# A second block whose gates and branch projections are computed token-first with 512-wide weight rows

## What is computed

```python
def mixer_block(h, ...):                      # h: 256 x 1024
    zin = h @ w_in                            # ... the last 4096 columns are the gates
    ...
    branches = jnp.stack([o_a, o_b, o_c, o_d], axis=2)      # four of 256 x 256
    proj = jnp.einsum('bsnw,nwd->bsnd', branches, w_branch) # four of 256 x 1024
    gate = jax.nn.sigmoid(gates).reshape(b, s, N_BRANCH, D_MODEL)
    merged = jnp.sum(gate * proj, axis=2)                   # 256 x 1024
    return merged @ w_out
```

## Time and profile before

| | us |
|---|---|
| median of 3 runs (lowest, highest) | 2224.96 (2223.97, 2225.07) |
| profiled execution: span | 2222.8 |
| TensorE busy (share of the span) | 2189.5 (99%) |
| weight loads of TensorE (overlap its matmuls) | 2006.0 (90%) |
| VectorE busy | 1458.6 (66%) |
| ScalarE busy | 1114.8 (50%) |
| GpSimd busy | 52.3 (2%) |

### The profile page before, as it was taken

How to read it: one execution, slowest core, us unless ns; L and a number is a source line. 1 busy time by engine, 2 the same in 40 slices (tenths; PEclk the granted TensorE clock), 3 DMA queues, 4 the chain that set the end, 5 groups by cost and what they waited for, 6 DMA issues and landing times.

```text
span 2222.8 us, 36553 instructions
## 1 busy us (share of the span) xinstructions
PE 2189.5 (99%) x15888; PEld 2006.0 (90%) x15888; DVE 1458.6 (66%) x1616; ACT 1114.8 (50%) x1419; POOL 52.3 (2%) x46
## 2 busy tenths in 40 slices
PE   8999999999999999999999999999999999999998
PEld 7999998888899999788799999988889999998887
DVE  5778567555768757666677867456657786745664
ACT  5555645454564564544465445444445553544443
POOL 0000000000000000000000000000000000000000
PEclk9999999999999999999999999999999999999999
DMA  7645455565564555556545444456555544445553
GB/s 233 181 139 168 148 200 171 189 200 190 180 187 137 158 181 174 173 186 228 178 136 140 146 134 170 146 165 201 200 175 155 152 134 144 160 159 164 189 200 113
DMA packets 288614, 376.97 MB, mean 170 GB/s; under 512 B 22335, under 2 KB 240517, under 8 KB 288454
## 3 DMA queue, kind: packets, MB, share of 16 engines
q1 hardware_dynamic: 288454, 374.62, 53.2%
HBM read 368.10 MB, written 1.05 MB: 166 GB/s over the span
## 4 chain that ended last, share of the span: by engine, by line
PE 91%; DVE 6%; ACT 2%; issue 1%; DMA 1%; SPq 0%; POOL 0%; DVEq 0%; POOLq 0%; ACTq 0%
PE ps L611 17%; PE ps L2246 14%; PE ps L2817 7%; PE ps L621 5%; PE ps L2267 5%; PE ps L2257 4%; PE ps L1009 4%; PE ps L921 4%; PE ps L2325 4%; PE ps L623 3%; PE ps L2269 2%; PE ps L676 2%; PE ps L635 2%; PE ps L2314 2%; PE ps L961 1%; PE ps L937 1%
## 5 line engine op out<-in xcount | busy, mean ns | idle before, releaser
L1305 DVE TENSOR_TENSOR a_wlo<-a_ring,a_whi 128x2048 fp32r<-128x2048 f32 (+1 forms) x173 | 393.0, 2274 | 101.9 <-ACT a_whi L1035 101.4
L3152 DVE TENSOR_TENSOR b_wlo<-b_ring,b_whi 128x2048 fp32r<-128x2048 f32 (+1 forms) x168 | 379.6, 2262 | 109.6 <-ACT b_whi L2842 109.0
L1035 ACT CAST a_whi<-a_ring 128x2048 fp32r<-128x2048 f32 (+1 forms) x173 | 328.0, 1899 | 141.2 <-PE ps L921 48.7
L611 PE MATMUL ps<-a_nsp,a_whi 128*128 128x256 f32 x2144 | 387.3, 283 | 0.0
L2842 ACT CAST b_whi<-b_ring 128x2048 fp32r<-128x2048 f32 (+1 forms) x168 | 317.2, 1889 | 124.7 <-PE ps L2817 79.0
L611 PEld LDWEIGHTS ps<-a_nsp,a_whi 128*128 128x128 f32 x2144 | 334.1, 192 | 0.2
L611 PE MATMUL ps<-a_nsp,a_wlo 128*128 128x256 f32 x1072 | 306.3, 286 | 0.0
L2246 PE MATMUL ps<-b_nsp,b_whi 128*128 128x256 f32 x1568 | 284.7, 283 | 0.0
L2246 PEld LDWEIGHTS ps<-b_nsp,b_whi 128*128 128x128 f32 x1568 | 244.0, 191 | 0.1
L2246 PE MATMUL ps<-b_nsp,b_wlo 128*128 128x256 f32 x784 | 227.9, 291 | 0.9 <-DVE b_wlo L3152 0.9
L611 PEld LDWEIGHTS ps<-a_nsp,a_wlo 128*128 128x128 f32 x1072 | 205.5, 192 | 1.6 <-issue 1.0
(11 more groups left out here) (580 smaller groups left out, 4224.4 us busy)
## 6 DMA issues: line engine op xcount, KB each, us to landing
b_ring<-in_w_in SPq DMA_DIRECT2D x50, 1024.0 KB, 5.9
a_ring<-in_w_in SPq DMA_DIRECT2D x49, 1024.0 KB, 5.4
a_ring<-in_w_ffn_in SPq DMA_DIRECT2D x44, 1024.0 KB, 5.1
a_ring<-in_w_gate SPq DMA_DIRECT2D x32, 1024.0 KB, 5.5
b_ring<-in_w_up SPq DMA_DIRECT2D x32, 1024.0 KB, 5.4
b_ring<-in_w_down SPq DMA_DIRECT2D x32, 1024.0 KB, 5.0
a_ring<-in_w_ffn_out SPq DMA_DIRECT2D x22, 1024.0 KB, 4.9
a_ring<-in_w_branch SPq DMA_DIRECT2D x16, 1024.0 KB, 5.1
```

Of the source, the lines that this page charges most:

```text
L611: mm = T.matmul(out, w[:, k, c:c + P], x_[:, k, :], start=k == 0 and n == 0, stop=k == KD - 1 and n == 2)
L1035: nc.scalar.copy(part(whi, h), part(ring, h)).then_inc(hi_ok, 1)
L1305: nc.vector.tensor_tensor(part(wlo, h), part(ring, h), part(whi, h).bitcast(F32), ALU.subtract).then_inc(lo_ok, 1)
L3152: nc.vector.tensor_tensor(part(wlo, h), part(ring, h), part(whi, h).bitcast(F32), ALU.subtract).then_inc(lo_ok, 1)
```

## The change

The gates and the branch projections are computed token-first: the activations (128 tokens) are stationary and the weights move, 512 columns a matmul. `gates` and `merged` are now token-first, [128, 2 token tiles, 1024 features], in the same places. Two gate parts make a chunk of 512 gate columns: the first holds rows 0 to 511 of the weights, the second rows 512 to 1023, and both token tiles accumulate over the two parts in the two banks (`gate_rows`). ScalarE evicts both tiles behind the second. Of a branch, m now counts 512-column halves times token tiles. The sum is turned by TensorE (`merged_turn`, eight transposes for each half of the features), and its high and low pieces are read from PSUM. The memory's sixteen transposes move from behind part 30 into the output projection, in two groups of eight, behind its parts 1 and 2 (`memory_turn`).

```diff
-GATE_AT = {h: g for g, h in enumerate([*range(12, 20), *range(21, 25), *range(26, 30)])}
+GATE_AT = {h: (g // 2, g % 2) for g, h in enumerate([*range(12, 20), *range(21, 25), *range(26, 30)])}
...
-            parts += [(8, 256, lambda l, g=GATE_AT[h]: cols(a["w_in_2"], l, GATE2 + 256 * g, 256))]
+            parts += [(4, 512, lambda l, c=GATE2 + 512 * GATE_AT[h][0], r=GATE_AT[h][1]:
+                       rows(a["w_in_2"], l, 4 * P * r, 4)[:, :, c:c + 512])]
...
+        else:
+            c, r = GATE_AT[h]
+            used += [(full, filled["gate", c, 1]) if r else (half_used, c + 1)]
...
+        def gate_rows(h):
+
+            g, r = GATE_AT[h]
+            hi, lo = both(h)
+            pe.wait_ge(lo_ok, h + 1)
+            for t in range(NT):
+                if t:
+                    mid(h)
+                b = bank(("gate", g, t))
+                for kk in range(4):
+                    k = 4 * r + kk
+                    for j, (x_, w) in enumerate(((nlo, hi), (nhi, lo), (nhi, hi))):
+                        mm = T.matmul(b, x_[:, k, t * P:(t + 1) * P], w[:, kk, :],
+                                      start=k == 0 and j == 0, stop=k == KD - 1 and j == 2)
+                if r:
+                    mm.then_inc(full, 1)
+            if not r:
+                mm.then_inc(half_used, 1)
...
             for m in range(4):
+                half, t = m // 2, m % 2
                 if m == 2:
                     mid(h)
+                if n == 3 and m == 3:
+                    merged_turn(0)
                 b = bank(("br", n, m))
+                for k in range(2):
+                    for j, (x_, w) in enumerate(((y_lo, hi), (y_hi, lo), (y_hi, hi))):
+                        mm = T.matmul(b, x_[:, k, t * P:(t + 1) * P], w[:, k, half * 512:(half + 1) * 512],
+                                      start=k == 0 and j == 0, stop=k == 1 and j == 2)
+                mm.then_inc(full, 1)
+
+        def merged_turn(half):
+
+            pe.wait_ge(mg_ok, 10 + 2 * half)
+            for m in (2 * half, 2 * half + 1):
                 for i in range(2):
-                    c = (2 * m + i) * P
-                    for k in range(2):
-                        for j, (w, x_) in enumerate(((lo, y_hi), (hi, y_lo), (hi, y_hi))):
-                            mm = T.matmul(b[:, i * SEQ:(i + 1) * SEQ], w[:, k, c:c + P], x_[:, k, :],
-                                          start=k == 0 and j == 0, stop=k == 1 and j == 2)
-                mm.then_inc(full, 1)
+                    for t in range(NT):
+                        c = (2 * m + i) * P
+                        mm = T.transpose(ps[:, 4 + m, i * SEQ + t * P:i * SEQ + (t + 1) * P],
+                                         merged[:, t, c:c + P], ident)
+                mm.then_inc(mg_turned, 1)
+
+        def memory_turn(half):
+
+            pe.wait_ge(ml_ok, 2 * half + 2)
+            pe.wait_ge(xn_ok, 8)
...
             if h == 30:
                 b_turn(3)
-                turned(1, 4)
...
             residual_rows(H_OUT2 + i, i, 1)
+            if i == 0:
+                merged_turn(1)
+            if i == 1 or i == 2:
+                memory_turn(i - 1)
...
+        def evict_gate(g, func):
+
+            for t in range(NT):
+                act.wait_ge(full, filled["gate", g, t])
+                A.activation(gates[:, g // 2 % 2, t, g % 2 * 512:g % 2 * 512 + 512], ps[:, unit["gate", g, t] % 2, :], func
+                             ).then_inc(free_a, 1)
...
         def merged_hi(m):
-            act.wait_ge(mg_ok, m + 9)
-            A.copy(nhi[:, 2 * m:2 * m + 2, :], merged[:, 2 * m:2 * m + 2, :]).then_inc(mh_ok, 1)
+            act.wait_ge(mg_turned, m + 1)
+            A.copy(nhi[:, 2 * m:2 * m + 2, :], ps[:, 4 + m, :].rearrange("p (a b) -> p a b", a=2)).then_inc(mh_ok, 1)
...
-            if i == 31:
-                act.wait_ge(pr_free, 12)
-                turned(1, 4, QE, memhi)
-        for m in range(4):
-            merged_hi(m)
-        for i in range(H_OUT2, H_WK):
-            hi(i + 2)
+        merged_hi(0)
+        merged_hi(1)
+        hi(H_OUT2 + 2)
+        merged_hi(2)
+        merged_hi(3)
+        hi(H_OUT2 + 3)
+        hi(H_WK)
+        act.wait_ge(pr_free, 12)
+        turned(1, 4, QE, memhi, range(4))
+        turned(1, 4, QE, memhi, range(4, KD))
+        hi(H_WK + 1)
...
             if i == 31:
-                gated(3, 0)
-                gated(3, 1)
+                for m in range(4):
+                    gated(3, m)
                 merged_lo(0)
-                gated(3, 2)
-                gated(3, 3)
                 merged_lo(1)
         lo(H_OUT2 + 1)
+        lo(H_OUT2 + 2)
         merged_lo(2)
         merged_lo(3)
-        lo(H_OUT2 + 2)
-        turned(1, 4, QE, memhi, memlo, range(8))
         lo(H_OUT2 + 3)
         lo(H_WK)
+        turned(1, 4, QE, memhi, memlo)
```

More of the change, by code:

```diff
@@ L1978, in second_block @@
     for h in range(FEW2, H_OUT2):
-        order += [("br", BRANCH_AT[h], m) for m in range(4)] if h in BRANCH_AT else [("in", h)]
+        if h in BRANCH_AT:
+            order += [("br", BRANCH_AT[h], m) for m in range(4)]
+        elif h not in GATE_AT:
+            order += [("in", h)]
+        elif GATE_AT[h][1] == 0:
+            order += [("gate", GATE_AT[h][0], t) for t in range(NT)]
     unit = {key: n for n, key in enumerate(order)}
@@ L1989, in second_block @@
     used = [(cq_used, 1), (cq_ps, 2)]
-    used += [(full, filled[("br", BRANCH_AT[h], 3) if h in BRANCH_AT else ("in", h)]) for h in range(FEW2, H_OUT2)]
+    for h in range(FEW2, H_OUT2):
+        if h in BRANCH_AT:
+            used += [(full, filled["br", BRANCH_AT[h], 3])]
+        elif h not in GATE_AT:
+            used += [(full, filled["in", h])]
+        else:
+            c, r = GATE_AT[h]
+            used += [(full, filled["gate", c, 1]) if r else (half_used, c + 1)]
     used += [(out_used, i + 1) for i in range(3)] + [(res_ps, 2)]
@@ L2871, in mlp_hi, with turned @@
                     ins.then_inc(nhi_ok, 1)
-        def turned(r, b0, gain, dst_):
-            for k in range(KD):
+        def turned(r, b0, gain, dst_, ks=range(KD)):
+            for k in ks:
                 if k % 2 == 0:
@@ L2887, in evict_cq, with evict @@
                 A.copy(cqk[:, t, :], ps[:, 2 + t, 0:384]).then_inc(cq_out, 1)
[L2889 removed]
+        def evict_gate(g, func):
+            for t in range(NT):
+                act.wait_ge(full, filled["gate", g, t])
+                A.activation(gates[:, g // 2 % 2, t, g % 2 * 512:g % 2 * 512 + 512], ps[:, unit["gate", g, t] % 2, :], func
+                             ).then_inc(free_a, 1)
+        def evict(h):
             act.wait_ge(full, filled["in", h])
@@ L3499, in gated @@
             i = 4 * n + m
-            b = ps[:, unit["br", n, m] % 2, :].rearrange("p (a b) -> p a b", a=2)
-            gt, out = gates[:, n % 2, 2 * m:2 * m + 2, :], merged[:, 2 * m:2 * m + 2, :]
+            t, cols_ = m % 2, slice(m // 2 * 512, m // 2 * 512 + 512)
+            b = ps[:, unit["br", n, m] % 2, :]
+            gt, out = gates[:, n % 2, t, cols_], merged[:, t, cols_]
             if m == 0:
-                dve.wait_ge(*((sig_ok, 1), (sig_ok, 2), freed[unit["in", 24]], freed[unit["in", 29]])[n])
-            if n == 1 and m == 3:
-                dve.wait_ge(*freed[unit["in", 19]])
+                dve.wait_ge(*((sig_ok, 1), (sig_ok, 2), freed[unit["gate", 4, 1]], freed[unit["gate", 6, 1]])[n])
+            if n and m == 2:
+                dve.wait_ge(*freed[unit["gate", 2 * n + 1, 1]])
             dve.wait_ge(full, filled["br", n, m])
```

48 lines of the change are left out of this document (27 added, 21 removed).

## The result

The changed kernel takes **2232.86 us** (median of 5 runs, 2231.04 to 2233.80) against 2225.07 us (5 runs, 2223.97 to 2225.78) of the kernel before in the same job: ratio 1.0035, 95% interval 1.0024 to 1.0046, slower by 7.8 us. The prediction said 2226.2, with no change (less than 0.2%) as the likeliest outcome; the measured change is 0.35%. The time lies at the far end of the range of 2220 to 2233, beyond the forecast's own bounds (2221.4 to 2230.2), and close to what the rival with the clock gave (2233). The profiled execution took 2231.04 us with a span of 2229.0, 6.2 more than the span before.

The account below looks back on a forecast made before the run. TensorE's own instructions were taken to set the time: 6.45 us lost less 5.85 gained is +0.6 a layer, +1.2 in two, giving a span of 2224.0 and, with 2.2 for the median, 2226.2 us; range 2220 to 2233.

Parts of the forecast that it names:

- the rival with the clock: Part 31 and projection: TensorE's waits make its clock fall, 3.4 us lost a layer, 2233 us; chance 0.12.
- the first two rivals: TensorE loses the clock, 2233 us, chance 0.12; other engines hold parts 12 to 30, 2232 us, chance 0.15.
- held parts 12 to 30 at the old pace: Gates and branches: other engines' chains close half the gaps, 2.9 us a layer lost, 2232 us; chance 0.15.
- Fewer starts save nothing: Gate parts: still 5.81 us each in the new form, the 6.46 us gain gone, 2239 us; chance 0.02.
- the columns' pace: Gate parts: 512-wide stream runs without the 14 ns, 5.14 us a part, 2213.7 us; chance 0.04.
- The gain of the gate parts: Parts 12 to 30: nineteen parts save 6.46 us, less 0.18 and 0.43, net 5.85 us a layer.
- 48 x 0.1210 = 5.81: A gate part before: 48 matmuls of 256 columns at 0.1210 us, the average of 72 starts, 5.81 us.
- Chain (a): Middle of part 19: VectorE feeds the inverse, so TensorE comes 0.16 us earlier, not 0.34; 0.18 lost.
- (b): Part 28 to part 31: VectorE's own chain limits the gain to 0.42 us where 0.85 is offered; 0.43 lost.
- The loss from part 31 on: Part 31 to the output projection's end: exposed transposes and idling make it 34.2 us for 27.75, 6.45 lost a layer.
- t = 0: Start of part 31, at 1344.59 before; forecast not to come earlier, TensorE idling some 1.6 us instead.
- The rival of the waits of part 31 not arising: Part 31: VectorE reaches the last products early enough, 3.1 us of idling not paid, 2220.0 us; chance 0.09.

Follow-up runs that it names:

- cut experiments: One needless 128-column product added in the middle of each half of each gate part: changed kernel then 2243.97 us, kernel before then 2231.76 us.
- the run with the memory turn alone: Kernel before with only the 16 memory transposes moved from behind part 30 to behind the output projection's second and third parts: 2230.38 us, ratio 1.0027.
- the two kernels with fillers: Changed kernel with 16 or 8 useless transposes in each of the two idle stretches, before part 31 and before the output projection: 2228.02 and 2228.53 us.
- VectorE's queue reordered: Changed kernel with early branch turn, early first low half, half the memory turn in part 31, and VectorE's weight split and low half reordered around gating: 2219.28 us.
- the early turn: Changed kernel with the fourth branch's input turned in the middle of part 30, its low half ahead of the third branch's last two gating steps: 2228.28 us.
- the run with 8 fillers: Changed kernel with 8 useless transposes in each of the two idle stretches, before part 31 and before the output projection: 2228.53 us.
- the changed kernel with cuts: Changed kernel with one needless 128-column product added in the middle of each half of its gate parts: 2243.97 us, ratio 1.0083 to the kernel before.

## Why the prediction was right or wrong

**The number.** The forecast of 2226.2 was 6.7 us too low, and 2232.86 is inside the range only because the range was drawn out to the first two rivals as priced. That the rival with the clock gave 2233 is luck in part: it added 6.8 us of clock to a sum in which the rest was 2 to 3 us too low, and the clock costs about 4.

**The bound and the shape of the sum: right.** TensorE's stream sets the time, and no other engine held parts 12 to 30 at the old pace, which was one rival. No new wait for an eviction shows there. *Fewer starts save nothing* and *the columns' pace* are out too: the wide starts lie 0.228 us apart, as forecast. For the gap rule of the Trainium skill (TensorE: Matmul & The Clock Gate, "Back-to-back issue gap"), with its 215.8 ns at 512 columns, the trace gives 12 ns more.

**The gain of the gate parts: mis-sized, 4.34 for 5.85.** It is the step "48 x 0.1210 = 5.81". The 72 starts of the earlier trace rows hold the first matmul behind a run of small ones, which takes 0.20 us (1327.54 to 1327.74) in place of 0.12, and the average spreads that over the pace. From TensorE's timeline before, in the middle of part 30:

```profile
1340.33 0.28 PE L2314 MATMUL ps<-b_ylo,b_whi 128*128 128x256 f32 x1
...
1341.89 0.28 PE L2314 MATMUL ps<-b_yhi,b_whi 128*128 128x256 f32 x1
```

13 steps in 1.56 us are 0.120 each. A part then saves 48 x 0.120 - 24 x 0.228 = 0.29 us, nineteen 5.5 where 6.46 were forecast. The measured 4.34 also lies below the bound of 4.9 that the sum used for the gain (which the 5.7 to 7.4 of the working, less 0.18 and 0.43, do not give: that is 5.1 to 6.8). The same stretch after, compared with the earlier trace rows, has the same extra at its head: 0.32 to the second start, then 34 steps in 7.75 us, 0.228 each.

```profile
1322.87 0.48 PE L2326 MATMUL ps<-b_whi,b_nsp 128*128 128x512 f32 x1
1323.19 0.39 PE L2326 MATMUL ps<-b_wlo,b_nsp 128*128 128x512 f32 x1
...
1330.94 0.39 PE L2326 MATMUL ps<-b_whi,b_nsp 128*128 128x512 f32 x1
1331.16 0.39 PE L2349 MATMUL ps<-b_whi,b_ylo 128*128 128x512 f32 x1
```

The rest is a cost that the prediction had at zero: the ends of the streams. Small products break parts 12 to 30 into 28 streams a layer in both kernels, and with the 0.036 us of the cut experiments 28 of them cost 1.0 more in the wide form. The two traces agree without that detour: the 28 streams take 113.3 us before and 108.8 after, which is 3.9 and 4.8 more than their starts at 0.120 and 0.228, so the ends cost 0.9 more. 5.5 - 1.0 = 4.5; the time between the streams grew by 0.2, and that leaves 4.3 of the measured 4.34. Chain (a)'s loss lies inside one of the streams, so this count is good to 0.2 or so. Both chains held. (a): TensorE went from the middle of part 18 to the inverse in 5.87 us, 0.08 less than before, where 0.16 were forecast. (b): from the middle of part 28 to part 31 it is 16.58 us in place of 17.05 (1327.54 to 1344.59), 0.47 gained where 0.42 were; the last piece of it, from the last branch's turn to part 31, grew from 2.57 us to 2.81.

**The loss from part 31 on: right, 6.59 for 6.45.** Its waits came as 0.58 us for the sum (0.8 forecast) and 2.20 for the low half (2.3). The wait before t = 0 was 2.21 us for a forecast of 1.6, and that figure was wrong on its own rows: the earlier trace rows leave 1344.59 - 1342.62 = 1.97 between the end of the branch's turn and part 31, and 1.97 is what the run with the memory turn alone shows. The moved memory turn, priced at 1.75 us, measured 1.80 alone. Work and waits together make +2.25 us a layer instead of +0.6: 4.5 in two.

**The clock: the step that failed.** The forecast took it to stay at 1.00 and gave its fall 0.12, with the words "none is as long". The condition, "if one wait, or the three of 1.6, 0.8 and 2.3 together, reach what that one did", was too strict for the one wait: single waits of 1.88 to 2.24 us were enough in half of the places. And it was not added up for the three, which make 4.7 us, more than 3.85. The earlier trace rows show that 3.85 us are enough; they don't show that less is safe. The kernel before has waits of 1.63 us without a fall and none near 2.2. Its mechanism was right, its cost partly: not one fall of 6.8 us at half pace but up to two a layer of 3.4 us, 2.5 us a layer with what a later wait absorbs. It adds 2.5 us to the profiled execution and about 4 in the mean of the executions (3.4 to 4.1, against the two kernels with fillers), more than the 3.0 from the gate parts. The Trainium skill (TensorE: Matmul & The Clock Gate, "The HAM clock gate") has the idle array falling to the lower level; the traces agree, with the addition that equal idling led to a fall in one layer and not in the other.

**The rival of the waits of part 31 not arising** was false as built, but true as an edit: with VectorE's queue reordered they all but vanish, and the kernel comes to 2219.28, near the 2220.0 that the rival gave. That the figures meet is a coincidence: this kernel also hides half of the memory turn, and gains less in the gate parts than the rival assumed.

## What to carry to other kernels

When work is moved out of a place where TensorE would wait, price the idling that it leaves as well as the work itself: moving 1.8 us of transposes a layer cost 5.4 us in two layers, and in the changed kernel useless transposes in the idle places won back about 4. Take a stream's pace from its inner starts alone, and price its ends apart, once for each place where small work cuts it. And when one wait is removed, look at which engine set it; the early turn moved 2.2 us of waiting and shortened the stretch by 0.25 only, because VectorE's queue behind it was as long as before. The moves in and around that queue took some 13 us off the changed kernel, more than the 7.8 that the change had cost.

## What the runs showed of the hardware

- The granted clock fell to 0.50 in 11 of 22 places with a single idle stretch of 1.88 to 2.24 us between long busy runs, each time for 3.4 us, in some layers and not in others with the same stretches (1.97 us twice, one fall). When it fell varies: in the changed kernel 1.2 and 0.7 us after the work had resumed (idle until 1339.45, starts 0.43 apart from 1340.77 on), in the kernel before with the memory turn moved as soon as it resumed (clock 0.51 from 1899.11 to 1901.11), in the changed kernel with cuts once 0.2 us before. No fall was seen behind 39 stretches of 1.62 to 1.67 us, nor behind the four of 1.24 to 1.36 us in the run with 8 fillers.
- A 128-column product in the middle of a stream costs 0.100 us between 256-wide matmuls and 0.136 us between 512-wide ones.
- The first matmul behind a run of small ones takes 0.08 us more to the next start at 256 columns (0.20 against 0.12) and 0.09 at 512 (0.32 against 0.228).
